# The 24 gate blocks of an input projection in 12 pairs of seven quarter products

## The reference

```python
h = rmsnorm(x, g_norm[l, 0])
q, k, v, su, sv, pc, gate = split_columns(h @ w_in[l])
ya = window_sink_attention(q, k, v, attn_sinks[l])
yb = spatial_gating(su, sv, g_sgu[l], w_spatial[l], b_spatial[l])
yc = multiscale_pool(pc, w_pool[l], pool_scale[l])
branches = jnp.stack([ya, yb, yc], axis=2)
proj = jnp.einsum('bsnc,ncd->bsnd', branches, w_branch[l])
gates = jax.nn.sigmoid(gate.reshape(B, S, N_BRANCH, D_MODEL))
merged = jnp.sum(gates * proj, axis=2)
x = x + rmsnorm(merged @ w_out[l], g_norm[l, 1])
```

## Time and profile before

| | |
|---|---|
| median of three executions | 1558.01 us (1553.12 to 1563.17) |
| profiled execution, its time | 1562.59 us |
| its span | 1560.8 us |
| PE busy | 1466.6 us, 94% |
| DVE busy | 897.8 us, 58% |
| ACT busy | 328.3 us, 21% |
| POOL busy | 32.0 us, 2% |
| mean granted clock of TensorE | 0.959 |

### The profile page before, as it was taken

How to read it: one execution, slowest core, us unless ns; L and a number is a source line. 1 busy time by engine, 2 the same in 40 slices (tenths; PEclk the granted TensorE clock), 3 DMA queues, 4 the chain that set the end, 5 groups by cost and what they waited for, 6 DMA issues and landing times.

```text
span 1560.8 us, 30115 instructions
## 1 busy us (share of the span) xinstructions
PE 1466.6 (94%) x12742; PEld 1322.8 (85%) x12742; DVE 897.8 (58%) x1783; ACT 328.3 (21%) x657; POOL 32.0 (2%) x47
## 2 busy tenths in 40 slices
PE   7999999989999969998889999999998889999997
PEld 6888788889999836777787999989998778999997
DVE  2141133347864481466554777886685546887865
ACT  1132104140000111420112122220101652222201
POOL 0130000000000000000000000000001100000000
PEclk9999999999999989999998999999998668999999
DMA  8434244246544402321000344444443002444442
GB/s 338 152 122 158 68 148 149 97 126 205 176 174 163 162 0 99 118 70 42 4 4 2 112 139 155 162 146 173 169 162 135 1 1 96 147 162 152 147 163 81
DMA packets 54479, 190.42 MB, mean 122 GB/s; under 512 B 6961, under 2 KB 9137, under 8 KB 53970
## 3 DMA queue, kind: packets, MB, share of 16 engines
q1 hardware_dynamic: 50480, 180.67, 33.7%
q10 hardware_dynamic: 3874, 7.92, 1.6%
HBM read 187.51 MB, written 1.05 MB: 121 GB/s over the span
## 4 chain that ended last, share of the span: by engine, by line
PE 87%; DVE 8%; issue 3%; ACT 1%; DMA 0%; POOL 0%; DVEq 0%; ACTq 0%; SPq 0%; PEldq 0%; POOLq 0%
PE ps L1799 86%; DVE arena L1551 1%; DVE arena L1574 1%; DVE arena L1602 1%; DVE arena L1717 0%; DMA ring<-in_stream 0%; DVE rs L2255 0%; DVE arena L1601 0%; DVE arena L792 0%; DVE arena L1721 0%; DVE arena L790 0%; DVE arena L1340 0%; DVE arena L1332 0%; DVE res L2264 0%; DVE arena L1330 0%
## 5 line engine op out<-in xcount | busy, mean ns | idle before, releaser
L1799 PE MATMUL ps<-arena,ring 128*128 128x136 f32 (+3 forms) x4816 | 864.0, 333 | 18.0 <-DMA ring<-in_stream 8.1
L1799 PEld LDWEIGHTS ps<-arena,ring 128*128 128x128 f32 x4816 | 752.0, 193 | 103.1 <-issue 19.9
L1799 PE MATMUL ps<-arena 64*64 64x64 f32 (+8 forms) x6748 | 572.0, 263 | 45.9 <-DVE arena L1730 12.2
L1799 PEld LDWEIGHTS ps<-arena 64*64 64x64 f32 (+3 forms) x6748 | 504.1, 165 | 88.0 <-issue 44.6
L790 DVE TENSOR_TENSOR arena<-ring 128x512 f32<-128x512 f32 x92 | 63.3, 688 | 95.1 <-PE ps L1799 93.6
L1799 PE MATMUL ps<-arena,consts 128*128 128x16 f32 (+10 forms) x384 | 90.4, 391 | 8.5 <-DVE arena L1721 4.8
L1551 DVE SCALAR_TENSOR_TENSOR arena<-arena,cols 128x271 f32<-128x271 f32 (+1 forms) x176 | 84.0, 498 | 11.2 <-ACT arena L1226 8.1
L1799 PEld LDWEIGHTS ps<-arena,consts 128*128 128x128 f32 (+3 forms) x384 | 70.5, 231 | 22.2 <-DVE arena L1721 4.9
L777 ACT COPY arena<-ps 128x136 f32<-128x136 f32 (+1 forms) x64 | 17.2, 268 | 323.1 <-PE ps L1799 323.1
L1226 ACT ACTIVATE arena<-arena,cols 128x272 f32<-128x272 f32 x88 | 49.2, 606 | 125.0 <-DVE arena L1484 70.3
L792 DVE TENSOR_TENSOR arena<-arena,ring 128x512 f32<-128x512 f32 x92 | 63.7, 693 | 3.2
(11 more groups left out here) (270 smaller groups left out, 896.6 us busy)
## 6 DMA issues: line engine op xcount, KB each, us to landing
ring<-in_stream SPq DMA_DIRECT2D x342, 512.0 KB, 3.7
consts<-in_consts ACTq DMA_DIRECT2D x1, 1580.0 KB, 8.7
arena<-in_x_t ACTq DMA_DIRECT2D x1, 1024.0 KB, 5.8
arena<-in_mem_t ACTq DMA_DIRECT2D x1, 1024.0 KB, 4.8
res<-in_x_t ACTq DMA_DIRECT2D x1, 1024.0 KB, 14.6
out_t<-arena SPq DMA_DIRECT2D x4, 256.0 KB, 2.5
arena<-in_g ACTq DMA_DIRECT2D x1, 640.0 KB, 5.8
arena<-in_w ACTq DMA_DIRECT2D x2, 256.0 KB, 4.7
```

Source lines behind the costliest of these rows:

```text
L1799: return nc.tensor.matmul(out, lhs, rhs, start=start, stop=stop)
```

## The change

The 24 gate blocks (18 to 41 of the stream) are run as 12 pairs in seven products. PE issues pairs 0 to 3 where the first 8 blocks were and pairs 4 to 11 where the 16 blocks were. The seven products of a pair lie in two banks (`TIGHT`), pairs taking turns between banks 0, 1 and 2, 3. VectorE forms the token sums and the weight sums of pairs 0 and 1 behind the q evacuations and ahead of the memory's norm. `gate_quads(i)` forms the result quarters of pair i and then the weight sums of pair i + 2; it stands between the pieces of the attention: pairs 0 to 3 behind the `sv` scaling, 4 and 5 each behind one normalising, 6 to 11 behind the norm of `sv`. ScalarE copies each first product and takes one sigmoid of 128 x 512 for a pair (`gate_up`). PE asks for all 24 gates (`ev["gate"]`) at the same place as before, ahead of the transposes of `sv`. The new buffers lie over places that are free at that time.

```diff
+        TIGHT = {7: (0, 0), 5: (0, 1), 4: (0, 2), 3: (0, 3), 6: (1, 0), 2: (1, 1), 1: (1, 2)}
+        GATES = 12
         SEVEN, n_pairs, n_groups, n_sums = {}, 0, 0, 0
-        for name, y, sums in (("upq", Seven(FIRST["up"], P, [4], (3, 0), WIDE_UP, UH // 2, FF // 2, -UH, True), 1),
...
+        XSUM["gate"] = [merged.rearrange("p n t -> p (n t)")[:, 512 * n:512 * (n + 1)].rearrange(
+            "p (k t) -> p k t", k=4) for n in range(4)]
+        WSUM["gate"] = [arena[:, a:a + 2048].rearrange("p (n k m) -> p n k m", n=4, k=4)
+                        for a in (gates_at + 24 * S + 24 * P, keys_at)]
+        QUADS["gate"] = [arena[:, a:a + 1024].rearrange("p (n t) -> p n t", n=8) for a in (lora_at, lora_at + 1024)]
...
-            act.wait_ge(products, 3 * y.pair(i) + (3 if y.place.get(2) == (2, 2) else 1))
+            act.wait_ge(products, 3 * y.pair(i) + (3 if y.place[2][0] == y.place[1][0] else 1))
...
-            pe.sem_inc(ev["gate"], GB)
-            tiles("gate", FIRST["in"] + 18, 8, h, S)
+            for i in range(4):
+                seven_products(pe, mm, "gate", only=i)
...
-            tiles("gate", FIRST["in"] + 26, 16, h, S, j0=8)
+            for i in range(4, GATES):
+                seven_products(pe, mm, "gate", only=i)
...
-            pe.wait_ge(ev["gate"], GB + 24)
+            pe.wait_ge(ev["gate"], 2 * GATES)
...
-            for j in range(8):
-                act.wait_ge(used, b + 18 + j + 1)
-                f(gates[:, j, :], ps[:, j % GB, 0:S], ACT.Sigmoid).then_inc(ev["gate"], 1)
+
+            def gate_up(i):
+                act.wait_ge(ev["gate"], 2 * (i + 1))
+                f(gates[:, 2 * i:2 * i + 2, :].rearrange("p a (b t) -> p (a b) t", b=2), QUADS["gate"][i % 2][:, 4:8, :],
+                  ACT.Sigmoid).then_inc(gates_up, 1)
+            keep_first_product(act, "gate", 0)
+            for i in range(1, 4):
+                keep_first_product(act, "gate", i)
+                gate_up(i - 1)
 
             act.wait_ge(at_m, 1)
             for e in range(8):
                 link(f(sc1[:, e, :], sc1[:, e, :], ACT.Exp, bias=small[:, 16 + e:17 + e],
                        accum_out=small[:, 24 + e:25 + e]))
             f(small[:, 32:40], small[:, 32:40], ACT.Exp).then_inc(at_p, 1)
+            keep_first_product(act, "gate", 4)
+            gate_up(3)
             act.wait_ge(at_m, 2)
             for e in range(8):
                 link(f(sc0[:, e, :], sc0[:, e, :], ACT.Exp, bias=small[:, 40 + e:41 + e],
                        accum_out=small[:, 48 + e:49 + e]))
             f(small[:, 56:64], small[:, 56:64], ACT.Exp).then_inc(at_p, 1)
             root(6, S, scale=2.0, which=3)
-            with act.Fori(0, 2) as it:
-                for s in range(8):
-                    act.wait_ge(used, it * 8 + (b + 26 + s + 1))
-                    f(gates[:, bass.ds(it * 8 + (8 + s), 1), :], ps[:, s % GB, 0:S],
-                      ACT.Sigmoid).then_inc(ev["gate"], 1)
+            for i in range(5, GATES):
+                keep_first_product(act, "gate", i)
+                gate_up(i - 1)
+            gate_up(GATES - 1)
...
+            dve.wait_ge(normed, 1)
+            x_sums(link, tt, "gate")
+            weight_sums(dve, tt, "gate", 0, 0)
+            weight_sums(dve, tt, "gate", 1, 0)
+
+            def gate_quads(i):
+                y = SEVEN["gate"]
+                q = QUADS["gate"][i % 2]
+                p1, u2, uv, quarters = q[:, 0, :], q[:, 1, :], q[:, 2:4, :], q[:, 4:8, :]
+                two = lambda p: product_at(y, i, p, 2).rearrange("p (a t) -> p a t", a=2)
+                dve.wait_ge(used, y.block(i + 1))
+                dve.wait_ge(p1_kept, y.pair(i) + 1)
+                link(tt(u2, p1, product_at(y, i, 6), ALU.add))
+                if i >= 2:
+                    dve.wait_ge(gates_up, i - 1)
+                tt(quarters[:, 2, :], p1, product_at(y, i, 2), ALU.add)
+                link(tt(uv, two(7), over(u2, 2), ALU.add))
+                tt(quarters[:, 0:4:3, :], uv, two(4), ALU.add)
+                tt(quarters[:, 1, :], uv[:, 0, :], product_at(y, i, 5), ALU.add).then_inc(ev["gate"], 2)
+                if i + 2 < GATES:
+                    weight_sums(dve, tt, "gate", i + 2, 0)
             dve.wait_ge(ld_s, 16 * 5)
...
                     link(tt(sv, sv, col_wide("g_sgu", 0, 4, S), ALU.mult))
+                    for i in range(4):
+                        gate_quads(i)
...
                 tt(sc, sc, tot.unsqueeze(2).to_broadcast([P, 8, nk]), ALU.mult).then_inc(at_n, 1)
+                gate_quads(4 + r)
             dve.wait_ge(rooted, 3)
             link(v.reciprocal(rs[:, 0:S], rs[:, 0:S]))
             tt(sv, sv, over(rs[:, 0:S], 4), ALU.mult).then_inc(arms_dve.sem, 1)
+            for i in range(6, GATES):
+                gate_quads(i)
```

More of the change, by code:

```diff
@@ L319, in program @@
         at_t, at_tc = sem("at_turned"), sem("at_turned_copied")
+        gates_up = sem("gates_up")
         arms_pe = Steps(sem("arms_pe"), "sgu_turned:1 pool_out:1 sgu_out:1 att_out:1")
@@ L347, in program @@
         WIDE_UP = {7: (0, 0), 5: (0, 1), 4: (0, 2), 3: (0, 3), 6: (1, 0), 2: (1, 1), 1: (2, 0)}
+        TIGHT = {7: (0, 0), 5: (0, 1), 4: (0, 2), 3: (0, 3), 6: (1, 0), 2: (1, 1), 1: (1, 2)}
+        GATES = 12
         SEVEN, n_pairs, n_groups, n_sums = {}, 0, 0, 0
-        for name, y, sums in (("upq", Seven(FIRST["up"], P, [4], (3, 0), WIDE_UP, UH // 2, FF // 2, -UH, True), 1),
+        for name, y, sums in (("gate", Seven(FIRST["in"] + 18, P, [4], (0, 2), TIGHT, 0, GATES, 0, True), 1),
+                              ("upq", Seven(FIRST["up"], P, [4], (3, 0), WIDE_UP, UH // 2, FF // 2, -UH, True), 1),
                               ("down", Seven(FIRST["down"], P, [4] * 4, (4, 0), SPLIT, 0, 4, 0, True), 4),
@@ L463, in program @@
             XSUM[name], WSUM[name], QUADS[name] = square_x[name == "sb_q"], square_w, square_q
-        SRC["upq"] = h.rearrange("p (k b) t -> p k b t", b=2)
+        SRC["gate"] = SRC["upq"] = h.rearrange("p (k b) t -> p k b t", b=2)
         XSUM["upq"] = [arena[:, y1_at + 512 * n:y1_at + 512 * (n + 1)].rearrange("p (k t) -> p k t", k=4)
@@ L1928, in _ @@
             pe.wait_ge(pl_y, 1)
+            pe.wait_ge(gates_up, GATES)
             pe.sem_inc(ev["branch"], GB)
```

## The result

The change took 1551.88 us, the median of 20 executions (1543.51 to 1560.62), and the kernel before 1561.48 us, the median of 20 beside it (1551.56 to 1566.10). The ratio is 0.9949 with an interval of 0.9930 to 0.9969: 8.0 us faster, between 4.8 and 10.9. A second comparison, of 12 executions with 17, gave 0.9970 (0.9947 to 0.9993), 4.7 us. These are the recorded ratios, not those of the medians, which lie 9.60 us apart in the first comparison and 6.95 in the second. The forecast was 1551.7 us and 6.3 us faster.

A forecast was written before the change was run, and what follows sets the result against it. PE, busy 94% of the span, was taken to bound the kernel. Saving 8.0 us there, less waits of 0.5, 0.6 and 0.6, gave -6.3 us and 1551.7 us against the median of 1558.01; range 1545 to 1560.

The forecast's parts named there:

- Seven products cost 6.25 us a pair: Gate stage on PE: pairs run at the up projection's pace, twelve cost 75.0 us, saving 8.0 us.
- the rival that rested on them: Each small matmul waits for its weight load: a pair 10.8 us, kernel 1605 us; 2% together with one other rival.
- VectorE ahead of the stage is covered: Some 8 us of token and weight sums before the gate stage fit VectorE's idle 23.2 us: cost 0, bound 2 us.
- Pair 2 waits 0.5 us: PE waits at pair 2's product 6 for VectorE's second weight sum, beside GpSimd: 0.5 us, between 0.3 and 2.2.
- Pair 8 waits 0.6 us: PE wants pair 8's second weight sum at 135.2, VectorE has it at 135.7: 0.6 us of wait.
- The schedule: Pair-by-pair times of PE, VectorE and ScalarE in the gate stage; second softmax ends at 123.5, last pair at 159.8 or so.
- The hand-over costs 0.6 us: Gate stage to arms: PE stands 0.45 us ahead of the transposes of `sv` and some 0.15 ahead of L1905.
- Sum: Whole kernel: -8.0 + 0.5 + 0.6 + 0.6 = -6.3 us.
- The absolute number: Whole kernel: forecast 1551.7 us, set against the earlier kernel's median of 1558.01 us; chance 66%.
- The clock in the arms: Rival: the arms' half clock, costing about 3.4 us, vanishes (1548.3 us) or comes as much earlier; 9%.
- VectorE as the bound: Rival: VectorE bounds the gate stage from pair 2 to 9, adding 3 us, 1554.7 us; 17%.
- the late softmax: Rival: second softmax on ScalarE ends at 128, PE stops about 4 us at pair 7 or 8, 1558.8 us; 6%.

The follow-up runs named there:

- eight-pair experiment: Changed kernel with its first eight gate blocks run the old way, only pairs 4 to 11 in seven products; 1555.94 us, timed once, stage 80.99 us.
- the loaded kernel: Changed kernel with four more 128x512 additions on VectorE in each pair's work; 1559.68 us, timed once, gate stage 89.17 us.
- the late softmax: Changed kernel with eight more 128x512 copies on ScalarE ahead of the second softmax; 1556.95 us, timed once, gate stage 84.26 us.
- wide bias matmuls: Changed kernel with spatial gating's eight bias matmuls as two of 512 columns: 1542.05 us, once; with quarters 0 first as well: median 1546.85 us.

## Why the prediction was right, step by step

- **Seven products cost 6.25 us a pair.** Right for ten pairs; the first took 6.35 and pair 2, which waited, 6.89. The eight-pair experiment shows that the saving is there. The small matmuls' weight loads cost nothing beyond what the up projection's rows held, and the rival that rested on them is out. The figure of the Trainium skill (TensorE: Matmul & The Clock Gate, Back-to-back issue gap), about 81 ns at 128 columns where the bare formula gives 56, does not hold for this stream: a record takes 111.6 ns, twice 55.8.
- **VectorE ahead of the stage is covered.** Right, with 7.4 us left.
- **Pair 2 waits 0.5 us.** 0.64, for the two reasons given, both now shown apart. The contention was 0.9 us instead of some 0.2, and VectorE would have been in time without it. The prediction's other estimate, three waits and 2.2 us, did not come.
- **Pair 8 waits 0.6 us.** Wrong, it didn't wait. The schedule let ScalarE copy a first product behind the pair's end. The copy only needs products 1 and 2, and product 3 still runs for 0.9 us: pair 4's copy began at 114.58 and not behind 115.5. So the second softmax ended at 122.52 instead of 123.5, and all that VectorE has behind it came 1.0 to 1.2 us sooner: quarters 6 ended at 133.1 instead of 134.3, and the second sum of pair 8 at 134.45 instead of 135.7, 0.5 us ahead of PE's second product:

```profile
133.76 0.69 DVE L801 TENSOR_TENSOR arena<-arena,ring 128x512 f32<-128x512 f32 x1
```

```profile
134.93 1.95 PE L1808 MATMUL ps<-arena 128*128 128x128 f32 x16
```

- **The hand-over costs 0.6 us.** 0.16, for the same reason: quarters 11 began 0.2 us behind the pair's end (159.25 behind 159.05) and ended 1.8 behind it instead of 2.1. The 0.15 ahead of the later transposes didn't come.
- **Sum.** The gate stage and hand-over gave -7.05 us where the sum had -6.3: PE's pairs saved 8.05 us, and off that go 0.10 for the first pair, 0.64 for pair 2, 0.10 for the second scores and 0.16. Two comparisons of times gave -8.0 and -4.7; -7.05 is a ratio of 0.9955 and lies in both intervals.
- **The absolute number** came out closer than its parts deserve: the kernel before was at 1558.01 in three executions and at 1561.48 in twenty, so a better anchor would have made the forecast 1555.2. That the median then fell 0.2 us beside the forecast is luck.
- **The clock in the arms** was held a rival, as if there were one place for it. It is not an alternative to the forecast but a scatter on top: the arms took 20.19 us in the kernel before and 21.99, 20.33, 18.89, 20.53, 18.88, 20.52 and 23.76 in the seven profiles with the change's arms (the last with a wait of 1.67 us in it, the loaded kernel). In these eight the clock was low for 3.4 us in two, 6.8 in four and 10.2 in two, and the arms took 18.9, 20.2 to 20.5 and, the wait taken off, 22.0 to 22.1: longer by half of the low time. The 20 executions of the change have a mean granted clock between 0.954 (1560.62 us) and 0.965 (1543.51 us), with a correlation of -0.97 between clock and time. So the spread of a single time goes with how long the clock is low.
- **VectorE as the bound, and the late softmax**: neither happened. The loaded kernel and the late softmax show that both are possible and about how far off they were, a wait of at most 1.6 us at pair 7 being free.

What stays open: why the clock stays low in the arms for 3.4 us in one execution and 10.2 in another, which property of the chain of small matmuls brings the fall, and whether wide bias matmuls keep the clock high in every execution; two profiles show it.

## What to carry to other kernels

Cost a step from the same code at another place of the trace, here the up projection's pair, and spend the effort on the queues around it: which instruction of a busy engine each piece is behind, and when the waiting starts. Work for VectorE with two inputs from SBUF should not lie beside GpSimd's large additions where PE waits for it; moving GpSimd's work later moved the collision to a worse place. Where single runs scatter by more than the effect, compare stages between the same two instructions, at an equal granted clock, and use the times only for the sign.

## What the hardware showed that I had not expected

- VectorE's additions of 0.69 us took up to 2.27 us beside GpSimd's of 2.22, and GpSimd's own took 2.22 where it was 1.89.
- Behind a stop of PE of 3.34 us the granted clock fell from 2.4 to 1.2 GHz for about 3.4 us. It fell within a stop of 2.81 us and was low for 6.0 us of the work behind it. At the stop of 2.02 us ahead of the scores, in every one of these profiles, it did not fall.
- Eight matmuls of one row by 128 columns between eight products cost 8.4 us in all at mixed clock, 4.1 as two of 512 columns and the eight products together. The fall of the clock went with them, in both profiles, and the arms took 15.08 us instead of 18.9 to 22.0.
